# Opening of the trunk by pairs of channel tiles: one shift unit and one scale unit for each pair, and half weight blocks

## The chip, the cores and the metric

The kernel runs on one core of one Trainium2 chip. The metric is device microseconds of one execution, lower is better; the median of several runs is compared. Profiles come from one profiled execution. Engines: PE (TensorE, with PEld for its weight loads), DVE (VectorE), ACT (ScalarE), POOL (GpSimd) and SP (SyncE, which here only issues transfers).

## The reference

Two token groups (128 context tokens, 512 latent tokens) go through two layers. Only the opening of the first layer is touched:

```python
def layer(l, x, cvec, ctx_kv, ang):
    m = (jax.nn.silu(cvec) @ w_mod[l] + b_mod[l])[..., None, :]
    sh1, sc1, g1, sh2, sc2, g2 = jnp.split(m, N_MOD, axis=-1)
    h = _rmsnorm(x, norm1_g[l]) * (1 + sc1) + sh1
    q, k, v, bg, cg, xc = jnp.split(h @ w_in[l], SPLITS, axis=-1)
    q = _rmsnorm(q.reshape(bsz, n, N_HEADS, 2, HEAD_DIM), q_norm_g[l])
    ...
```

`D_MODEL` is 1024, that is, eight channel tiles of 128. `sh1` and `sc1` are the first two of six 1024-wide vectors that `w_mod` makes; `h` of a channel tile needs `sh1` and `sc1` of that tile.

## The kernel before

Each engine runs a program of its own, written out by hand in its final order, and they meet through counting semaphores (`wait_ge`, `then_inc`). Nothing is scheduled by a tool: what stands first on an engine runs first, and a wait holds all behind it.

All large products are made in float32 as three products of split numbers: a weight block is copied to `w_hi` by ACT (`split_hi_of`) and the rest, `raw - w_hi`, is written to `w_lo` by DVE (`split_lo_of`). A channel tile of `h` is split alike: DVE makes `hn` (x times gain times 1/rms, L1747), ACT adds the shift and makes `h_hi` (L1283), DVE makes `h_lo` (L1758). `norm_tiles(k0, k1)` does that for channel tiles k0 to k1-1 on DVE and `norm_hi(k)` on ACT. `h_ready` counts what is done, two steps to a tile.

`w_mod` comes in units of 256 columns (1 MB). Each unit covers two channel tiles. Units 0 to 3 make `sh1`, units 4 to 7 make `sc1`; they have their own buffers (`pre_w`, `mod_q`, by `PRE_SLOT`) and are loaded in the opening. A group of two units goes through these steps:

- PE: `mod_sum` for either unit, 8 matmuls each, into one PSUM bank (`mod_used` counts units);
- ACT: `rows`, the bank copied to `mod_row` (`row_read`);
- PE: `mod_turn`, four transposes back into the bank (`modT_full`);
- DVE: `mod_post`, a sum over four parts and the bias, into `modv` (`mod_ready`).

Before the change group 0 is units 0 and 1 (shift of channel tiles 0 to 3), group 2 is units 4 and 5 (scale of tiles 0 to 3), and groups 1 and 3 are the same for tiles 4 to 7. `PRE_ORDER` is 0, 2, 1, 3. Groups 0 and 2 are made before the first product; groups 1 and 3 between its steps.

The first product is the queries' part of `h @ w_in` (p = 0): 512 columns, five token tiles t, eight channel tiles k. `qkv_step` is three matmuls (L815 to L817) for one k and one t; five PSUM banks hold the sums of the five token tiles. Weight block 0 (slot 0) holds k = 0 to 3 and block 1 (slot 1) k = 4 to 7, 128x2048 each. For k = 0 to 3 the loop takes the five token tiles in turn. For k = 4 to 7 it takes t = 0 to 2, and then come whole `qkv_unit`s of four steps for t = 3 and t = 4. After k = 5 stands `first_pair_sum(0)`: the first two of the later `w_mod` units, from `mod_q`, with the row copy `rows(0, 0)` behind it on ACT and its turn (L729) between the units of t = 3 and t = 4. After t = 4 comes `first_pair_sum(1)`, whose first matmul waits until `mod_ready` is 5, that is, until DVE has made `mod_post(0, 0)`. On DVE that `mod_post` stands behind `split_lo(2)` (the keys' weight block 2) and behind the first item of the query norm (L1814 to L1845); on ACT the copy `split_hi(2)` stands behind `rows(0, 0)`. Then PE transposes `kc` (L883) and goes to the keys' part (p = 1).

Small rows (biases, gains, the convolution's weights, lambda and the rope tables) are issued by ACT's queue; PE transposes `vrow` and spreads `brow` (L795 to L798) before the first turn. POOL's queue loads the cached keys `kc` (L626), later the cached values, and in the MLP adds weight blocks (L636). SP's queue loads x, the `w_mod` units and the weight blocks in the order of its program.

## Time and profile before

| what | value |
|---|---|
| median of 3 runs | 1616.09 us (1615.43 to 1618.02) |
| profiled execution | 1615.98 us |
| its span, first to last instruction | 1614.2 us |
| PE busy | 1562.6 us, 97% |
| DVE busy | 1031.9 us, 64% |
| ACT busy | 727.3 us, 45% |
| mean granted TensorE clock | 0.99 |
| DMA in the first 40 us | 353 GB/s |

The profiled execution took 1.8 us more than its span. Times inside the trace are us from the span's start. The waits view says which engine stood idle and what ended it; the timeline gives, for merged rows, the start, the length, the engine and line, the tiles, the number of instructions, and in brackets the idle time before.

### The profile page before, as it was taken

How to read it: one execution, taken by the hardware profiler on the slowest of the kernel's cores; microseconds unless marked ns; L12 is line 12 of the kernel's file. 1: busy time of each engine (PE TensorE's matmuls, PEld its weight loads, DVE VectorE, ACT ScalarE, POOL GpSimd, SP SyncE). 2: the span in 40 equal slices, each digit the busy share in tenths (PEclk: the TensorE clock that was granted, in tenths of full speed). 3: DMA queues.
4: the chain of work that ended last, by engine and by line, in shares of the span. 5: the costliest groups of instructions: out<-in, count | busy, mean ns of one | idle time of the engine just before them, and what ended most of it. 6: DMA issues, size and time to landing. Idle time of an engine off the chain costs nothing. (4 is left out here: it accounts for less than half of the span.)

```text
span 1614.2 us, 26302 instructions
## 1 busy us (share of the span) xinstructions
PE 1562.6 (97%) x10543; PEld 1457.1 (90%) x10543; DVE 1031.9 (64%) x1654; ACT 727.3 (45%) x1216; POOL 142.6 (9%) x172
## 2 busy tenths in 40 slices
PE   5999999998999999999989999999899999999998
PEld 4777888987999999999977788889799999999998
DVE  5662666636775765757775537676587667476673
ACT  4543544325652643525443444533466355263451
POOL 0000000000211202112000000000022121120210
PEclk9999999999999999999989999999999999999999
DMA  9554011473866957759543531034088575694862
GB/s 353 183 189 164 27 53 35 149 253 87 190 150 151 216 136 167 180 150 219 156 147 111 170 105 53 28 104 131 3 196 186 146 184 147 160 211 135 193 152 82
DMA packets 284571, 236.13 MB, mean 146 GB/s; under 512 B 10464, under 2 KB 254752, under 8 KB 284448
## 3 DMA queue, kind: packets, MB, share of 16 engines
q1 hardware_dynamic: 259920, 189.82, 37.7%
q0 software_dynamic: 23680, 44.05, 15.9%
q8 instruction: 84, 1.38, 0.3%
q10 hardware_dynamic: 848, 0.56, 0.1%
q14 instruction: 39, 0.32, 0.1%
HBM read 188.78 MB, written 3.67 MB: 119 GB/s over the span
## 5 line engine op out<-in xcount | busy, mean ns | idle before, releaser
L636 POOL DMA_DIRECT2D raw_all<-raw_all x160 | 137.9, 877 | 1124.4 <-DMA raw_all<-in_w_up_dram 988.6
L1541 ACT ACTIVATE w_hi<-raw_all 128x1024 fp32r<-128x1024 f32 x120 | 126.1, 1056 | 234.9 <-DMA raw_all<-raw_all 116.1
L1154 PE MATMUL ps<-gg,w_hi 128*128 128x322 f32 x704 | 219.1, 311 | 0.0
L1156 PE MATMUL ps<-gg,w_lo 128*128 128x322 f32 x704 | 218.7, 311 | 0.0
L1155 PE MATMUL ps<-gg,w_hi 128*128 128x322 f32 x704 | 218.4, 310 | 0.0
L2077 DVE TENSOR_TENSOR w_lo<-raw_all,w_hi 128x1024 fp32r<-128x1024 f32 x120 | 146.5, 1221 | 109.8 <-ACT w_hi L1541 109.0
L1099 PE MATMUL ps<-hc_lo,w_hi 128*128 128x322 f32 x640 | 199.6, 312 | 0.0
L1101 PE MATMUL ps<-hc_hi,w_lo 128*128 128x322 f32 x640 | 198.9, 311 | 0.0
L1097 PE MATMUL ps<-hc_hi,w_hi 128*128 128x322 f32 x640 | 198.7, 310 | 0.0
L1097 PE MATMUL ps<-ht_hi,w_hi 128*128 128x322 f32 x480 | 150.7, 314 | 4.8 <-ACT s L1559 2.7
L1101 PE MATMUL ps<-ht_hi,w_lo 128*128 128x322 f32 x480 | 149.1, 311 | 0.0
L1099 PE MATMUL ps<-ht_lo,w_hi 128*128 128x322 f32 x480 | 149.0, 310 | 0.0
L1973 DVE SCALAR_TENSOR_TENSOR x<-ps,modv,x 128x128 f32<-128x128 f32 (+2 forms) x240 | 90.3, 433 | 91.5 <-PE ps L1156 54.1
L2038 DVE SCALAR_TENSOR_TENSOR tmp<-ub,vecs,tmp 128x642 f32<-128x642 f32 x168 | 139.3, 883 | 13.2 <-ACT tmp L1499 13.2
L1705 DVE TENSOR_TENSOR w_lo<-raw_all,w_hi 128x2048 fp32r<-128x2048 f32 x36 | 82.4, 2289 | 85.3 <-ACT w_hi L1267 85.3
L1156 PEld LDWEIGHTS ps<-gg,w_lo 128*128 128x128 f32 x704 | 132.9, 189 | 0.0
L1155 PEld LDWEIGHTS ps<-gg,w_hi 128*128 128x128 f32 x704 | 132.8, 189 | 0.0
L1154 PEld LDWEIGHTS ps<-gg,w_hi 128*128 128x128 f32 x704 | 132.5, 188 | 0.0
L686 PE MATMUL ps<-h_hi,w_hi 128*128 128x322 f32 x384 | 122.7, 320 | 0.0
L1097 PEld LDWEIGHTS ps<-hc_hi,w_hi 128*128 128x128 f32 x640 | 120.8, 189 | 0.0
L1101 PEld LDWEIGHTS ps<-hc_hi,w_lo 128*128 128x128 f32 x640 | 120.7, 189 | 0.0
L1099 PEld LDWEIGHTS ps<-hc_lo,w_hi 128*128 128x128 f32 x640 | 120.4, 188 | 0.0
(208 smaller groups left out, 3447.2 us busy)
## 6 DMA issues: line engine op xcount, KB each, us to landing
raw_all<-in_w_up_dram SPq DMA_DIRECT2D x280, 256.0 KB, 3.8
raw_all<-raw_all POOLq DMA_DIRECT2D x160, 256.0 KB, 4.0
raw_all<-in_w_in_dram SPq DMA_DIRECT2D x48, 512.0 KB, 4.8
raw_all<-in_w_mod_dram SPq DMA_DIRECT2D x48, 512.0 KB, 4.4
raw_all<-in_w_down_dram SPq DMA_DIRECT2D x16, 768.0 KB, 4.4
raw_all<-in_w_down_dram SPq DMA_DIRECT2D x16, 640.0 KB, 4.2
mod_q<-in_w_mod_dram SPq DMA_DIRECT2D x8, 1024.0 KB, 9.8
raw_all<-in_w_out_dram SPq DMA_DIRECT2D x16, 512.0 KB, 4.4
```

Source lines behind the costliest of these rows:

```text
L636: pool.dma_start(raw_f[:, BLK * dst:BLK * (dst + 1)], raw_f[:, BLK * src:BLK * (src + 1)], accum_op=ALU.add).then_inc(sum_full[which], 16)
L686: mm(out, wh[:, k, col:col + P], mov_hi(k), start=k == 0, stop=False)
L1097: mm(out, whi_f[:, c0:c0 + P], hh[:, k, slot, :], start=first and k == 0, stop=False, skip_group_check=not first)
L1099: mm(out, whi_f[:, c0:c0 + P], hl[:, k, slot, :], start=False, stop=False, skip_group_check=not first)
L1101: ins = mm(out, wlo_f[:, c0:c0 + P], hh[:, k, slot, :], start=False, stop=k == KH - 1, skip_group_check=not first)
L1154: mm(out, wh[:, k, :], gh, start=k == 0, stop=False)
L1155: mm(out, wh[:, k, :], gl, start=False, stop=False)
L1156: ins = mm(out, wl[:, k, :], gh, start=False, stop=k == kf - 1)
L1541: A(whi_b[:, 2 * i:2 * (i + 1), :], src, ACT.Copy).then_inc(up_hi[i], 1)
L1973: ins = V.scalar_tensor_tensor(out=xs, in0=ps[:, banks[h], p0:p0 + n], scalar=gate, in1=xs, op0=ALU.mult, op1=ALU.add)
L2038: return V.scalar_tensor_tensor(out=cen[:, s, 1:T - 1], in0=u[:, s, j:j + T - 2], scalar=vecs[:, l, w:w + 1], in1=cen[:, s, 1:T - 1], op0= ...
L2077: V.tensor_tensor(wlo_b[:, pair, :], raw_b[:, pair, :] if i else first_pair(g), whi_b[:, pair, :].bitcast(F32), ALU.subtract).then_inc(up_ ...
```

## The change

- The four opening groups are now by pairs of channel tiles: group h is unit h (shift) and unit 4 + h (scale) of tiles 2h and 2h + 1, all in one bank. `first_post(h)` on DVE takes the place of `mod_post` for them: two sums, one bias add.
- Only group 0 is made before the first product. Groups 1 to 3 have their sums after t = 2 of k = 0, 2, 4, and their turns after t = 1 of k = 1, 3, 5. Gains and `norm_tiles` go by two tiles.
- Weight block 0 comes as two halves (`first_part`), each split on its own (`part_split_hi`, `part_split_lo`, 128x1024); the first step needs only the first half.
- k = 0 to 5 take all five token tiles. For k = 6 and 7 the token tiles 0 to 2 come first, then `first_pair_sum(0)`, then tiles 3 and 4, the turn, and `first_pair_sum(1)`.
- Eight small rows stay on ACT's queue. Ten (convolution of the MLP, lambda, query and key gains) and the rope tables go to POOL's queue, ahead of `kc`; rope there waits for `hh_ready` 4.
- ACT loads the Sqrt table early, squares the context tokens before the latent ones have come, and makes the lambda exponential after all eight tiles.

```diff
-PRE_ORDER = [0, 2, 1, 3]
-PRE_BANKS = {0: 7, 2: 1, 1: 7, 3: 7}
-PRE_SLOT = {0: 0, 1: 2, 4: 1, 5: 3, 2: 4, 3: 5, 6: 6, 7: 7}
+PRE_SLOT = {0: 0, 4: 2, 1: 1, 5: 3, 2: 4, 6: 5, 3: 6, 7: 7}
...
             pre_load(0)
+            pre_load(4)
+            first_part(0)
             pre_load(1)
-            for u in (4, 5):
-                pre_load(u)
-            load(0, w_in_v, 0, KH, 0, QC)
-            for u in (2, 3, 6, 7):
-                pre_load(u)
+            pre_load(5)
+            first_part(1)
+            pre_load(2)
+            pre_load(6)
             load(1, w_in_v, KH, KH, 0, QC)
+            pre_load(3)
+            pre_load(7)
...
+            pool.wait_ge(const_ready, 2)
+            for l in range(DEPTH):
+                fr = ffn_conv_w[l].rearrange("w (t n) -> (w t) n", n=P)
+                pool.dma_start(vrow[:, l, 1, :], fr[0:P, :]).then_inc(rows_in, 16)
+                pool.dma_start(vrow[0:3 * V_FT - P, l, 2, :], fr[P:3 * V_FT, :]).then_inc(rows_in, 16)
+            for i, src in enumerate((lambda_q1, lambda_k1, lambda_q2, lambda_k2, q_norm_g, k_norm_g)):
+                pool.dma_start(brow[0:1, i * P:(i + 1) * P], src.rearrange("(a l) n -> a (l n)", a=1)
+                               ).then_inc(rows_in, 16)
+            pool.wait_ge(hh_ready, 4)
+            pool.dma_start(rope[:, :, :, :], rope_in).then_inc(rope_full, 16)
...
-            pre_sum(0)
+            mod_sum(None, 0, 0, None, None)
...
+            mod_sum(None, 0, 1, None, None)
+            spread(0, 0)
             mod_turn(None, 0)
-            pre_sum(2)
-            spread(0, 0)
-            mod_turn(None, 2)
...
+                    for k in range(KT - 2):
...
+                        for t in range(NT):
+                            normed(k, t)
+                            ins = qkv_step(k // KH, t, k % KH)
+                            if k % 2 == 0 and t == 2:
+                                pre_sum(k // 2 + 1)
+                            elif k % 2 and t == 1:
+                                mod_turn(None, k // 2 + 1)
...
+                    for t0, t1 in ((0, 3), (3, NT)):
+                        for k in range(KT - 2, KT):
+                            for t in range(t0, t1):
...
+                        if t0 == 0:
+                            first_pair_sum(0)
                     mod_turn(l, 0)
-                qkv_unit(1, 4)
-                first_pair_sum(1)
+                    first_pair_sum(1)
...
+            A(junk[:, 1:2], eps[:, :], ACT.Sqrt)
...
+            def first_post(h):
+                dve.wait_ge(modT_full, h + 1)
+                turned = ps[:, MOD_BANK, :].rearrange("p (v t q m) -> p v t m q", v=2, q=4, m=QUAD)
+                for vec in range(2):
+                    V.tensor_reduce(modv[:, vec, 2 * h:2 * h + 2, :], turned[:, vec, :, 0:2, :], axis=AX.X, op=ALU.add)
+                dve.drain()
...
-                    norm_tiles(4, KT)
+                    for k in range(0, KT, 2):
+                        if k:
+                            first_post(k // 2)
+                            dve.drain()
+                        gains(0, V_N1, k, k + 2)
+                        dve.drain()
+                        norm_tiles(k, k + 2)
+                        if k == 0:
+                            part_split_lo(1)
+                        elif k == 2:
+                            split_lo(1)
```

On PE, at the start of the first product, the rows before are these (the sums of groups 0 and 2 with the setup between them; L718 is a sum, L729 a turn, L750 the spread of 1/rms, L815 the first step):

```order
L718 MATMUL ps<-pre_w,cT 32x256 [waits pre_full0,cT_ready]
...
L718 MATMUL ps<-pre_w,cT 32x256 [waits pre_full1]
...
L795 MATMUL ps<-ident,vrow 128x128 [waits xT_read,ffn_in,small_in]
...
L729 MATMUL ps<-ident,mod_row 128x128 [waits row_read]
...
L718 MATMUL ps<-pre_w,cT 32x256 [waits pre_full4]
...
L718 MATMUL ps<-pre_w,cT 32x256 [waits pre_full5]
...
L815 MATMUL ps<-w_hi,h_hi 128x512 [waits h_ready,split_full0]
```

and with the change these (L733 is a sum, L744 a turn, L829 the first step):

```order
L733 MATMUL ps<-pre_w,cT 32x256 [waits pre_full0,cT_ready]
...
L810 MATMUL ps<-ident,vrow 128x128 [waits xT_read,rows_in,small_in]
...
L733 MATMUL ps<-pre_w,cT 32x256 [waits pre_full4]
...
L744 MATMUL ps<-ident,mod_row 128x128 [waits row_read]
...
L829 MATMUL ps<-w_hi,h_hi 128x512 [waits h_ready,part_lo]
...
L733 MATMUL ps<-pre_w,cT 32x256 [waits pre_full1,mod_ready]
```

One group of sums and one turn have gone behind the first step, and the setup's transposes wait for POOL's rows.

On PE, at the end of the queries' part, the rows before run from `first_pair_sum(0)` over 30 matmuls (k = 6 and 7 of t = 0 to 2, and the unit of t = 3), the turn and 12 matmuls (the unit of t = 4) to `first_pair_sum(1)` and the transposes of `kc` (L883):

```order
L718 MATMUL ps<-mod_q,cT 32x256 [waits mod_ready,modq_full0]
...
L729 MATMUL ps<-ident,mod_row 128x128 [waits row_read]
...
L815 MATMUL ps<-w_hi,h_hi 128x512
...
L718 MATMUL ps<-mod_q,cT 32x256 [waits mod_ready,modq_full2]
...
L883 MATMUL ps<-ident,kc 128x128 [waits kv_in]
```

and with the change only the steps of t = 3 and 4 (12 matmuls) and the turn stand between the two sums:

```order
L733 MATMUL ps<-mod_q,cT 32x256 [waits mod_ready,modq_full0]
...
L829 MATMUL ps<-w_hi,h_hi 128x512 [waits h_ready]
...
L744 MATMUL ps<-ident,mod_row 128x128 [waits row_read]
L744 MATMUL ps<-ident,mod_row 128x128 x3
L733 MATMUL ps<-mod_q,cT 32x256 [waits mod_ready,modq_full2]
...
L913 MATMUL ps<-ident,kc 128x128 [waits kv_in]
```

42 matmuls of the product stood between the two sums, 12 do now; the other 30 are ahead of the first sum.

On ACT the rows around `rows(0, 0)` before are

```order
L1217 ACTIVATE mod_row<-ps 128x512 [waits mod_used]
L1267 ACTIVATE w_hi<-raw_all 128x2048 [waits unit_done0,raw_full0]
L1326 ACTIVATE sq<-ps 128x512 [waits qkv_full]
L1329 ACTIVATE qraw<-ps 128x512
L1331 ACTIVATE st<-st,eps 128x8 [waits qsum_ready]
```

and with the change

```order
L1332 ACT_TABLE_LOAD
L1332 ACTIVATE lam_s<-lam_s 128x4 [waits lam_ready]
L1333 ACT_TABLE_LOAD
L1333 ACTIVATE junk<-eps 128x1
L1246 ACTIVATE mod_row<-ps 128x512 [waits mod_used]
L1290 ACTIVATE w_hi<-raw_all 128x2048 [waits unit_done0,raw_full0]
L1358 ACTIVATE sq<-ps 128x512 [waits qkv_full]
```

The copy of weight block 2 still stands behind the row copy; the lambda exponential and its two table loads have come in front of both.

## Rows read from the trace of the kernel before

**Rows 1.** Page, part 1: busy time, share and count of instructions.

```profile
PE 1562.6 (97%) x10543; PEld 1457.1 (90%) x10543; DVE 1031.9 (64%) x1654; ACT 727.3 (45%) x1216; POOL 142.6 (9%) x172
```

**Rows 2.** Waits of PE, 100 to 1614 us: total, times, longest.

```profile
PE ps L937 <- ACT probs L1386: 4.7, 4, 1.4
```

**Rows 3.** Timeline of PE before the first product: start, length, instruction, count.

```profile
18.66 0.88 PE L795 MATMUL ps<-ident,vrow 128*128 128x128 f32 x6
...
20.95 0.66 PE L729 MATMUL ps<-ident,mod_row 128*128 128x128 f32 x4
...
24.07 1.60 PE L750 MATMUL ps<-sq,ones 128*128 128x128 f32 x12
25.52 0.60 PE L729 MATMUL ps<-ident,mod_row 128*128 128x128 f32 x4
32.65 0.77 PE L815 MATMUL ps<-w_hi,h_hi 128*128 128x512 f32 x1 [6.53 <-DVE h_lo L1758]
```

**Rows 4.** Timeline of DVE: last opening memset, copies of x, first tiles.

```profile
2.37 0.06 DVE L1663 MEMSET eps<- 128x1 f32 x1
...
13.50 3.08 DVE L1678 COPY x<-ps 128x512 f32<-128x512 f32 x5
...
26.15 0.19 DVE L1650 TENSOR_REDUCE modv<-ps 128x8 f32<-128x32 f32 x1 [2.59 <-PE ps L729]
...
27.04 1.13 DVE L1747 SCALAR_TENSOR_TENSOR hn<-x,gain,ps 128x128 f32<-128x128 f32 x3
...
31.11 1.12 DVE L1747 SCALAR_TENSOR_TENSOR hn<-x,gain,ps 128x128 f32<-128x128 f32 x3
```

**Rows 5.** Page, part 5: a half block's low part, and a transfer issued by POOL.

```profile
L636 POOL DMA_DIRECT2D raw_all<-raw_all x160 | 137.9, 877 | 1124.4 <-DMA raw_all<-in_w_up_dram 988.6
...
L2077 DVE TENSOR_TENSOR w_lo<-raw_all,w_hi 128x1024 fp32r<-128x1024 f32 x120 | 146.5, 1221 | 109.8 <-ACT w_hi L1541 109.0
```

**Rows 6.** Line L626 (POOL's load of kc), last line of the answer.

```profile
DMA to landing us min/median/max: 6.6/6.6/6.6
```

**Rows 7.** Windows: length, busy time of PE, PEld, DVE, ACT, POOL, clock, DMA share, GB/s.

```profile
26.20:32.60 6.40, 0.00 (x0) 0.00 (x0) 5.43 (x18) 3.55 (x5) 0.00 (x0) 0.70 1.09 353
32.60:35.60 3.00, 2.95 (x7) 2.41 (x8) 3.00 (x8) 1.70 (x4) 0.00 (x0) 0.50 1.09 348
```

**Rows 8.** Timeline of PE in the first product.

```profile
50.06 0.60 PE L729 MATMUL ps<-ident,mod_row 128*128 128x128 f32 x4
...
54.13 0.47 PE L815 MATMUL ps<-w_hi,h_hi 128*128 128x512 f32 x1 [0.69 <-DVE h_lo L1758]
...
58.49 1.93 PE L718 MATMUL ps<-mod_q,cT 128*32 128x256 f32 x32
...
67.41 0.60 PE L729 MATMUL ps<-ident,mod_row 128*128 128x128 f32 x4
...
70.74 1.93 PE L718 MATMUL ps<-mod_q,cT 128*32 128x256 f32 x32
```

**Rows 9.** Timeline of ACT: the row copy of the first pair sum, and weight block 2.

```profile
60.49 0.60 ACT L1217 ACTIVATE mod_row<-ps 128x512 f32<-128x512 f32 x1 [2.08 <-PE ps L718]
60.99 1.91 ACT L1267 ACTIVATE w_hi<-raw_all 128x2048 fp32r<-128x2048 f32 x1
```

**Rows 10.** Timeline of DVE: weight block 2, mod_post(0, 0) and mod_post(0, 1).

```profile
62.93 2.29 DVE L1705 TENSOR_TENSOR w_lo<-raw_all,w_hi 128x2048 fp32r<-128x2048 f32 x1 [2.88 <-ACT w_hi L1267]
...
68.69 0.17 DVE L1653 TENSOR_TENSOR modv<-modv,vecs 128x8 f32<-128x8 f32 x1
...
77.86 0.17 DVE L1653 TENSOR_TENSOR modv<-modv,vecs 128x8 f32<-128x8 f32 x1
```

**Rows 11.** Timeline of PE, 366 to 378 us: two units' sums at half clock, then at full.

```profile
369.93 3.49 PE L718 MATMUL ps<-mod_t,cT 128*32 128x256 f32 x32
...
374.97 1.93 PE L718 MATMUL ps<-mod_x,cT 128*32 128x256 f32 x32
```

**Rows 12.** Timeline of PE: the keys' part, its first sum.

```profile
79.62 1.07 PE L718 MATMUL ps<-raw_all,cT 128*32 128x256 f32 x16
```

More of the change, by code:

```diff
@@ L183 @@
 HALVES = 24
-N_SMALL = 15
+N_SMALL = 8
+N_ROWS = 10
 YT_BANKS = [6, 7, 0, 1, 3, 4, 2, 5, 6, 7]
@@ L189 @@
 MOD_BANK = 7
-PRE_ORDER = [0, 2, 1, 3]
-PRE_BANKS = {0: 7, 2: 1, 1: 7, 3: 7}
-PRE_SLOT = {0: 0, 1: 2, 4: 1, 5: 3, 2: 4, 3: 5, 6: 6, 7: 7}
+PRE_SLOT = {0: 0, 4: 2, 1: 1, 5: 3, 2: 4, 6: 5, 3: 6, 7: 7}
 def mod_bank(l, h):
-    if l is None:
-        return PRE_BANKS[h]
-    return 2 if h == GAP_A[l] + 1 else MOD_BANK
+    return 2 if l is not None and h == GAP_A[l] + 1 else MOD_BANK
 LAM_INIT = [0.8 - 0.6 * math.exp(-0.3 * i) for i in range(DEPTH)]
@@ L867, in _ @@
-                pe.wait_ge(split_full[1], usable(l, 1))
-                for k in range(KH, KT):
-                    for t in range(3):
-                        normed(k, t)
-                        ins = qkv_step(1, t, k - KH)
-                        if k == KT - 1:
-                            ins.then_inc(qkv_full, 1)
-                    if l == 0 and k == 5:
-                        first_pair_sum(0)
-                qkv_unit(1, 3)
-                if l == 0:
-                    mod_turn(l, 0)
@@ L1224, in _ @@
             act.wait_ge(const_ready, 2)
-            small = [(rope[:, :, :, :], rope_in)]
+            small = []
             for src, r0, n in ((b_mod, V_BMOD, 48), (norm1_g, V_N1, KT), (norm2_g, V_N2, KT),
@@ L1231, in _ @@
                               conv_w[:, j, :].rearrange("l (t n) -> t l n", n=P)))
-            for i, src in enumerate((lambda_q1, lambda_k1, lambda_q2, lambda_k2, q_norm_g, k_norm_g)):
-                small.append((brow[0:1, i * P:(i + 1) * P], src.rearrange("(a l) n -> a (l n)", a=1)))
             assert len(small) == N_SMALL
             A(junk[:, 0:1], eps[:, :], ACT.Silu)
-            for dst, src in small[:8]:
+            for dst, src in small:
                 act.dma_start(dst, src).then_inc(small_in, 16)
@@ L1267, in split_hi_of, with part_split_hi @@
                 A(w_hi[:, b, 0:size], raw[:, b, 0:size], ACT.Copy).then_inc(hi_done[b], 1)
+            def part_split_hi(s):
+                act.wait_ge(part_in[s], 16)
+                A(w_hi[:, 0, s * 2 * QC:(s + 1) * 2 * QC], raw[:, 0, s * 2 * QC:(s + 1) * 2 * QC], ACT.Copy
+                  ).then_inc(hi_done[0] if s else part_hi, 1)
             rows(None, 0)
-            rows(None, 2)
-            split_hi_of(0, 0)
+            part_split_hi(0)
             for l in range(DEPTH):
@@ L1289, in _ @@
                     norm_hi(k)
-                    if k == 3:
-                        if l == 0:
-                            rows(None, 1)
+                    if l == 0 and k == 1:
+                        part_split_hi(1)
+                        rows(None, 1)
+                    elif l == 0 and k == 3:
                         split_hi(1)
-                        if l == 0:
-                            act.wait_ge(lam_ready, 1)
-                            A(lam_s[:, :], lam_s[:, :], ACT.Exp).then_inc(lam_exp, 1)
-                            A(junk[:, 0:1], eps[:, :], ACT.Sqrt)
-                            rows(None, 3)
+                        rows(None, 2)
+                    elif l == 0 and k == 5:
+                        rows(None, 3)
+                    elif l and k == 3:
+                        split_hi(1)
                     elif l and k == 5:
@@ L1301, in _ @@
                 if l == 0:
+                    act.wait_ge(lam_ready, 1)
+                    A(lam_s[:, :], lam_s[:, :], ACT.Exp).then_inc(lam_exp, 1)
+                    A(junk[:, 0:1], eps[:, :], ACT.Sqrt)
                     rows(l, 0)
@@ L1715, in _ @@
             dve.drain()
-            mod_post(None, 0)
             for l in range(DEPTH):
@@ L1725, in _ @@
                             ).then_inc(lam_ready, 1)
-            mod_post(None, 2)
+            first_post(0)
             for l in range(DEPTH):
@@ L1737, in reciprocals, with part_split_lo @@
                     reciprocals_of(l, which)
+                def part_split_lo(s):
+                    dve.wait_ge(hi_done[0] if s else part_hi, 1)
+                    part = slice(s * 2 * QC, (s + 1) * 2 * QC)
+                    V.tensor_tensor(w_lo[:, 0, part], raw[:, 0, part], w_hi[:, 0, part].bitcast(F32), ALU.subtract
+                                    ).then_inc(split_full[0] if s else part_lo, 1)
                 def norm_tiles(k0, k1):
```

119 lines of the change are left out of this document (62 added, 57 removed).

## Prediction

> **What bounds the kernel now.** The page first: PE is busy 97% of the span, no other engine over 64% [rows 1]. So the time is PE's work plus PE's idle time, and each idle stretch has to be read for what ended it. In the waits of PE after 100 us all ten kinds are ended by ACT or DVE, none by a DMA; the kind that comes back below is one of the attention, 4.7 us in four waits [rows 2]. A delay put in early is therefore carried to the end, unless such a wait takes it up. The opening is where PE idles most: after its last turn at 25.52 it has nothing until the first step at 32.65, 6.53 us [rows 3]. The windows show what this does to the clock: the granted share falls to 0.70 within the idle 6.4 us, and the next 3.0 us run at 0.50 (1.2 GHz), 7 matmuls in 2.95 us, 0.42 each, where the pace at full clock is 0.233 [rows 7].
>
> That pace I take from the timeline of the product: the sum of `first_pair_sum(0)` starts at 58.49, lasts 1.93 (to 60.42), 30 matmuls fill the time to the turn at 67.41, so 6.99 / 30 = 0.233; and turn plus 12 matmuls take 70.74 - 67.41 = 3.33 us [rows 8].
>
> **The change, part by part.**
>
> *An earlier first step.* PE can begin the setup (transposes of small rows) when DVE has copied x, at 13.50 + 3.08 = 16.58, say 16.7 [rows 4]; before it began at 18.66, behind the second unit's sum. Setup to turn is 20.95 - 18.66 = 2.29 [rows 3], which gives 19.0. The scale unit's sum (half of 1.93, 0.97) ends at 20.0; the spread takes 25.52 - 24.07 = 1.45, ACT's row copy of 0.60 lies beside it; the turn (0.60) ends at 22.0 [rows 3, 8]. From DVE's first sum at 26.15 to the first step at 32.65 were 6.50 us. In them, between `hn` of tile 0 (27.04 + 1.13 = 28.17) and of tile 1 (31.11), lay 2.94 us for the low part of a whole weight block [rows 3, 4]. Half a block costs 1.22 [rows 5], 1.72 less; the extra short sum adds about 0.19 [rows 4]. 6.50 - 1.72 + 0.19 = 4.97, so the first step comes at 27.0: **-5.65 us**. PE idles 5.0 us before it, little less than 6.53, so I let the half clock behind it cost what it cost before.
>
> *The small rows.* PE asks for them at 16.7. POOL may start after DVE's memsets, at 2.5 [rows 4], and issues ten; at 0.877 us an issue, as in its other transfers [rows 5], the last is issued at 10.4, and at the 6.6 us that `kc` took to land in this same busy stretch [rows 6] it is there at 17.0: 0.3 us late, not added above. The bounds: nothing if they land faster; if the issues cost 1.3 us instead, the last lands at 2.5 + 9 x 1.3 + 6.6 = 20.8, 4.1 us late, and all behind it with it. I stay at nothing, since `kc` (128x512) is four times as large as the largest of them (128x128). What is queued behind on POOL (rope, `kc`) is wanted only at DVE's rope tables and at PE's transposes after 72 us.
> The Trainium skill (DMA: Bandwidth & Descriptors, Anatomy of one DMA) gives a GpSimd transfer 2.0 us plus its bytes at 436 GB/s; an estimate from that page puts the last row at 12.6 and this term at zero. It would give `kc` 2.6 us; the trace has 6.6, so here the rule is not what bounds it.
>
> *One more group inside the product.* Three groups' sums and turns now lie behind the first step, two before: 1.93 for the sums, 3.33 - 12 x 0.233 = 0.53 for the turn, **+2.5 us** [rows 8].
>
> *Waits at the borders of the pairs.* A turn started at 50.06 and the first step that needed it at 54.13: 4.07 us of bias add, gains, two `hn`, `h_hi` and the first `h_lo`, covered by 12 matmuls, with 0.69 idle left [rows 8]. The change has this path three times (before k = 2, 4, 6), 0.1 longer for the second short sum, and covers each with the turn (0.53) and 9 matmuls (2.10) only: 4.17 - 2.63 = 1.5 idle, three times 4.6. Before were 0.69 and 0.20 (the latter is a bank's wait that goes too): **+3.7 us**.
>
> So PE would ask for `first_pair_sum(1)` at 70.74 - 5.65 + 2.5 + 3.7 = **71.3**: the gain at the front is already given back, with 0.6 on top.
>
> *The new wait.* `first_pair_sum(1)` waits for `mod_post(0, 0)`. Its chain is: sum (0, 0) ends at 60.42; ACT copies the row at 60.49 and weight block 2 at 60.99 for 1.91 [rows 9]; DVE takes the low part at 62.93 for 2.29, the first query item, and the bias add at 68.69 + 0.17 = 68.86 [rows 10]. That is 8.44 us. Before, 42 matmuls and a turn covered it (60.42 to 70.74, 10.3 us) and 1.9 us were left over. Now 12 matmuls and the turn stand there, 3.33 us [rows 8]. Queued behind the waiting matmul is the whole keys' part. The lambda exponential moved ahead on ACT is free: ACT has nothing else until the row. So PE waits 8.44 + 0.1 - 3.33 = **5.2 us** and starts the sum at 76.5, 5.8 later than 70.74.
>
> *Half clock behind it.* PE idled 6.53 us before and came back at 0.50; 5.2 us is near that, so I expect the same. Two units' sums took 3.49 at half clock and 1.93 at full, with the clock the only difference in the rows [rows 11]: **+1.5 us**. Whether some matmuls behind it are slow too is left to the range (7 were before, 0.2 each, 1.4). If the clock stays, the next check is `mod_post(0, 1)`: it ended at 78.03, 9.17 behind `mod_post(0, 0)` [rows 10], so now at 85.6, and PE asks for it at 79.62 + 5.8 = 85.4 [rows 12]: the delay is then 6.0, not less.
>
> **Sum:** -5.65 + 2.5 + 3.7 + 5.2 + 1.5 = +7.3 us. Against the profiled execution (1615.98, its span 1614.2 and 1.8 around it) that is 1623.3; the median of the runs is 0.1 higher, and on it I forecast **1623.4 us**.
>
> **The rivals.**
>
> 1. *The clock stays full after the new wait.* For it: 5.2 us is shorter than the idle time that lowered it. Against: the clock fell inside the 6.4 us window and not at its end [rows 7]. +6.0, 1622.1 us.
> 2. *The small rows come late* and the new bound of the opening is POOL's queue. For it: no row of before shows ten issues of POOL in a row. Against: the sizes. At 1.3 us an issue +7.3 + 4.1 = +11.4, 1627.5 us. The Trainium skill (SBUF — State Buffer, SBUF: two separate sides) says that DVE in a two-port mode keeps GpSimd from writing descriptors; no row here shows it, and it would be this rival's cause.
> 3. *Not slower: the attention takes the delay up.* PE waits there for ACT's exponentials, 4.7 us over both layers [rows 2]. If ACT's work in those places were late from its own backlog and not released by PE, a delay of PE would shrink these waits, at most by 4.7: +2.6, 1618.7 us. It decides only if nearly all of it is taken up, 4.1 of 4.7. Against: half of it lies in the second layer, and those exponentials follow PE's own scores.
> 4. *The change doesn't do what it says*, and the pairs' waits don't appear, because DVE gets through the path in less than 2.6 us: -4.6 in the forecast. The new wait stays, since its chain starts at the first sums: it moves with PE, so +2.7, 1618.8 us. Against: 4.07 us is measured. With no half clock too it would be faster than that by 1.5, and with some of rival 3 faster than before.
>
> **How the numbers follow.** Forecast 0.62, rival 1 0.14, rival 2 0.10, rival 3 0.06, rival 4 0.05, faster than before by any sum of these 0.03. Measurement tells 0.2%, 3.2 us, from no change. Slower: 0.62 + 0.14 + 0.10 = 0.86; same 0.11; faster 0.03. The range takes rival 1 and leaves room below it for a first step 1 to 2.5 us earlier than my 27.0, down to 1619.8, and takes rival 2 above: to 1627.8.
>
> **What would show it.** In the trace after: PE's first step near 27 (26 to 28), idle before it about 5; waits of about 1.5 before k = 2, 4 and 6, ended by DVE `h_lo`; one wait of about 5.2 on `modv` at about 71, with the bias add 8.4 behind the first sums; half clock behind it; `kc`'s transposes at about 80 in place of 72.6. Wrong at the front if PE waits for a DMA of `vrow` or `brow`; wrong at the end if PE passes `first_pair_sum(1)` with no wait, in which case I would find 1618 or less.

## The result, and the profile after

The changed kernel takes 1622.47 us (median of 7 executions, 1619.54 to 1626.92), the kernel before 1615.43 (7 executions): ratio 1.0046, 95% interval 1.0034 to 1.0058. The change costs 7.0 us. The forecast was 1623.4, slower by 7.3 than the median of 1616.1 known then.

The page of the changed kernel, its span and part 1 (compare [rows 1]):

```profile
span 1620.3 us, 26321 instructions
...
PE 1563.8 (97%) x10543; PEld 1457.4 (90%) x10543; DVE 1033.2 (64%) x1661; ACT 726.9 (45%) x1218; POOL 148.5 (9%) x183
```

Span less PE's busy time is 56.5 us; before it was 1614.2 - 1562.6 = 51.6. PE does the same 10543 matmuls, and 4.9 of the 6.1 us in the span are idle time. The waits of PE, 0 to 110 us (total, times, longest), say where:

```profile
PE ps L829 <- DVE h_lo L1806: 8.8, 4, 4.7
PE ps L793 <- DMA ident<-in_ident_dram: 8.8, 1, 8.8
PE ps L733 <- DVE modv L1695: 5.2, 1, 5.2
PE ps L810 <- DVE x L1720: 0.9, 1, 0.9
```

Behind 100 us nothing new waits; the attention's line of [rows 2] reads

```profile
PE ps L967 <- ACT probs L1418: 4.7, 4, 1.4
```

as before, so it took nothing up. The timeline of PE (start, length, instruction, count, idle before), for [rows 3], [rows 8] and [rows 12]:

```profile
17.49 0.84 PE L810 MATMUL ps<-ident,vrow 128*128 128x128 f32 x6 [0.89 <-DVE x L1720]
...
19.75 1.76 PE L733 MATMUL ps<-pre_w,cT 128*32 128x256 f32 x16
21.43 2.53 PE L765 MATMUL ps<-sq,ones 128*128 128x128 f32 x12
23.80 0.60 PE L744 MATMUL ps<-ident,mod_row 128*128 128x128 f32 x4
29.10 0.77 PE L829 MATMUL ps<-w_hi,h_hi 128*128 128x512 f32 x1 [4.71 <-DVE h_lo L1806]
...
42.21 0.47 PE L829 MATMUL ps<-w_hi,h_hi 128*128 128x512 f32 x1 [1.34 <-DVE h_lo L1806]
...
53.34 0.47 PE L829 MATMUL ps<-w_hi,h_hi 128*128 128x512 f32 x1 [1.44 <-DVE h_lo L1806]
...
64.41 0.51 PE L829 MATMUL ps<-w_hi,h_hi 128*128 128x512 f32 x1 [1.31 <-DVE h_lo L1806]
...
68.79 1.93 PE L733 MATMUL ps<-mod_q,cT 128*32 128x256 f32 x32
...
73.54 0.60 PE L744 MATMUL ps<-ident,mod_row 128*128 128x128 f32 x4
79.30 3.64 PE L733 MATMUL ps<-mod_q,cT 128*32 128x256 f32 x32 [5.16 <-DVE modv L1695]
82.87 1.12 PE L913 MATMUL ps<-ident,kc 128*128 128x128 f32 x4
```

The new wait stands at 74.14, 5.16 us long. DVE's side of it, for [rows 10], with the end of the setup for [rows 4]:

```profile
24.43 0.25 DVE L1675 TENSOR_REDUCE modv<-ps 128x4 f32<-128x16 f32 x2 [2.42 <-PE ps L744]
...
26.43 1.22 DVE L1784 TENSOR_TENSOR w_lo<-raw_all,w_hi 128x1024 fp32r<-128x1024 f32 x1
...
73.22 2.29 DVE L1747 TENSOR_TENSOR w_lo<-raw_all,w_hi 128x2048 fp32r<-128x2048 f32 x1 [6.36 <-ACT w_hi L1290]
...
78.98 0.17 DVE L1695 TENSOR_TENSOR modv<-modv,vecs 128x8 f32<-128x8 f32 x1
```

From the end of the first pair's sum (68.79 + 1.93 = 70.72) to 79.15 are 8.43 us. The windows (length, busy times, clock, DMA share, GB/s), for [rows 7], show the clock in the setup, in the first idle time and behind either wait:

```profile
17.40:20.00 2.60, 2.51 (x16) 1.47 (x20) 1.92 (x9) 0.00 (x0) 0.00 (x0) 1.00 1.09 385
20.00:23.40 3.40, 3.40 (x25) 2.38 (x18) 1.84 (x6) 1.54 (x2) 0.00 (x0) 0.50 1.09 393
```

```profile
24.40:29.10 4.70, 0.00 (x0) 0.03 (x1) 4.42 (x19) 1.90 (x4) 0.00 (x0) 0.76 1.09 360
29.10:33.30 4.20, 4.20 (x13) 2.88 (x17) 2.67 (x4) 1.29 (x2) 1.12 (x2) 0.50 1.07 386
...
79.30:84.80 5.50, 5.50 (x39) 3.28 (x40) 5.21 (x15) 2.04 (x5) 0.54 (x1) 0.50 0.16 56
```

**More is lost early than at the end.** The same instruction of both traces, three times: at the attention's first wait, in the output product of the first layer, and of the second. Before:

```profile
196.59 1.35 PE L937 MATMUL ps<-kT,qT 64*128 64x128 f32 x7 [0.98 <-ACT probs L1386]
```

```profile
389.24 0.42 PE L1073 MATMUL ps<-hc_hi,w_hi 128*128 128x322 f32 x1 [1.64 <-DVE hc_lo L2019]
```

```profile
1170.14 0.41 PE L1073 MATMUL ps<-hc_hi,w_hi 128*128 128x322 f32 x1 [1.63 <-DVE hc_lo L2019]
```

After:

```profile
207.75 1.34 PE L967 MATMUL ps<-kT,qT 64*128 64x128 f32 x7 [0.99 <-ACT probs L1418]
```

```profile
396.95 0.41 PE L1103 MATMUL ps<-hc_hi,w_hi 128*128 128x322 f32 x1 [1.62 <-DVE hc_lo L2069]
```

```profile
1175.62 0.41 PE L1103 MATMUL ps<-hc_hi,w_hi 128*128 128x322 f32 x1 [1.63 <-DVE hc_lo L2069]
```

The delay is 11.2 us, then 7.7, then 5.5. It began as two nearly equal parts: up to the point where the keys' part is under way (85 us before, 96.2 after, 470 matmuls in either) PE is busy for 66.85 and 72.56 us, so 5.7 us of the delay are slower matmuls and 5.5 us are idle time. Behind that point PE is idle for 33.4 us before and 32.9 after, so waits took up at most 0.5 us of it. The rest came back by the clock: the kernel before runs two stretches of PE at half clock, here in its windows,

```profile
295.10:298.40 3.30, 3.30 (x15) 3.30 (x14) 2.90 (x8) 2.50 (x3) 0.00 (x0) 0.50 0.02 5
370.20:373.50 3.30, 3.30 (x33) 1.45 (x25) 1.26 (x7) 0.34 (x2) 0.00 (x0) 0.50 0.00 0
```

and the changed kernel has the full clock from 290 to 400 us:

```profile
290.00:400.00 110.00, 104.42 (x826) 94.85 (x825) 61.42 (x117) 42.39 (x70) 0.35 (x1) 1.00 0.50 161
```

Half clock costs half of the 3.3 us of each window, so the two are 3.3 of the 3.5 us between the first and the second pair of rows. Of the next 2.2, 1.75 lie in the windows from 815 to 850 us, 0.80 against 0.85 of the full clock over 35 us:

```profile
815.00:850.00 35.00, 30.36 (x166) 25.50 (x165) 25.96 (x64) 14.19 (x23) 0.57 (x1) 0.80 0.28 90
```

```profile
815.00:850.00 35.00, 30.36 (x189) 26.68 (x188) 25.59 (x63) 15.70 (x23) 0.57 (x1) 0.85 0.44 142
```

(before, then after). By the end of the trace the difference is 6.1 us, the two spans' difference.

### The profile page after: what moved, and what is told of

The parts are those of the page before. It is cut to its first block and busy times, and to the rows that moved or that the text cites. A ratio compares the mean times of both kernels' runs of the same rounds, so it can differ in the third digit from the quotient of the medians.

```text
span 1620.3 us, 26321 instructions
## 1 busy us (share of the span) xinstructions
PE 1563.8 (97%) x10543; PEld 1457.4 (90%) x10543; DVE 1033.2 (64%) x1661; ACT 726.9 (45%) x1218; POOL 148.5 (9%) x183
```

## The experiments

Each is compared with executions of the kernel before on the same chip and in the same batch. The batches differ (the median of the kernel before is 1614.9 to 1617.2 in them), so kernels of different batches are compared by their ratios, not by their medians. PE's idle time is the span less its busy time in each trace; the clock is the mean of the granted share over all timed executions. The two rows that start with "and" add to "chain and turns early", the second of them to the first.

| kernel | ratio, 95% interval | median, us | PE idle, us | PE busy, us | clock |
|---|---|---|---|---|---|
| before | 1 | 1614.9 to 1617.2 | 51.6 | 1562.6 | 0.9907 (0.9904 to 0.9914 by batch) |
| changed | 1.0046 (1.0034 to 1.0058) | 1622.5 | 56.5 | 1563.8 | 0.9894 |
| changed, again | 1.0050 (1.0031 to 1.0068) | 1622.2 | 55.3 | 1564.8 | 0.9895 |
| before, end changed | 1.0042 (1.0030 to 1.0054) | 1622.5 | 56.4 | 1563.3 | 0.9892 |
| bias add first | 1.0049 (1.0035 to 1.0064) | 1624.2 | 54.7 | 1560.7 | 0.9903 |
| turns early | 1.0041 (1.0029 to 1.0053) | 1621.1 | 52.2 | 1569.7 | 0.9876 |
| both | 1.0038 (1.0025 to 1.0051) | 1622.0 | 52.4 | 1570.1 | 0.9884 |
| chain early | 1.0024 (1.0004 to 1.0043) | 1620.2 | 52.8 | 1562.8 | 0.9895 |
| chain and turns early | 1.0005 (0.9991 to 1.0019) | 1616.2 | 49.2 | 1564.3 | 0.9895 |
| and low part early | 0.9995 (0.9982 to 1.0009) | 1614.8 | 49.1 | 1563.6 | 0.9902 |
| and three moves more | 0.9982 (0.9971 to 0.9992) | 1614.3 | 50.3 | 1563.8 | 0.9910 |
| rows on ACT | 1.0053 (1.0037 to 1.0070) | 1624.3 | 56.4 | 1564.0 | 0.9892 |
| idle time filled | 1.0048 (1.0029 to 1.0067) | 1623.3 | 51.5 | 1565.2 | 0.9917 |
| filled, again | 1.0044 (1.0027 to 1.0061) | 1622.3 | 50.7 | 1569.4 | 0.9917 |

### One part alone: the new end in the kernel before

```diff
-                for k in range(KH, KT):
-                    for t in range(3):
...
-                    if l == 0 and k == 5:
-                        first_pair_sum(0)
-                qkv_unit(1, 3)
...
+                    for k in range(KH, KT - 2):
+                        for t in range(NT):
...
+                    for t0, t1 in ((0, 3), (3, NT)):
...
+                        if t0 == 0:
+                            first_pair_sum(0)
+                    mod_turn(l, 0)
```

> The kernel before, with only the end of the queries' part taken from the change: k = 4 and 5 with all five token tiles, k = 6 and 7 with t = 0 to 2, then first_pair_sum(0), t = 3 and 4, the turn and first_pair_sum(1). Theory (the new wait comes from that order alone): 12 matmuls and a turn, 3.3 us, stand against a chain of 8.4, so PE waits about 5.1 us for mod_post(0, 0), the sums behind it run at half clock (3.5 instead of 1.93), and the median rises by 5 to 7 us over the kernel before. Rival (the wait needs the opening by pairs, or a delay here is taken up later): PE waits under 2 us, or the median rises by under 3 us.

Ratio 1.0042, 6.8 us. Its timeline of PE has the wait and the half clock behind it to the hundredth of those in the changed kernel:

```profile
76.89 3.64 PE L718 MATMUL ps<-mod_q,cT 128*32 128x256 f32 x32 [5.16 <-DVE modv L1665]
```

The theory holds. This order alone costs as much as the whole change; the opening by pairs, with its first step 3.6 us earlier and its extra group and border waits, gains nothing in sum.

### The bias add first, the turns early, and both

The first kernel moves one call on DVE:

```diff
+                    mod_post(l, 0)
                 split_lo(2)
...
                         if t == 1 and p == 0:
-                            if l == 0:
-                                mod_post(l, 0)
                             rope_tables()
```

> The changed kernel, with DVE's mod_post(0, 0) ahead of split_lo(2) and of the first query item instead of behind them; all else as changed. Theory (the new wait is DVE's order, and it and the half clock behind it go through to the end): the bias add comes about 0.6 us behind the turn (which ends at 74.14), so the wait of 5.16 us falls to about 0.6, the sums of first_pair_sum(1) take 1.93 instead of 3.64, the transposes of kc come about 6.5 earlier (76.3 instead of 82.87), and the median falls by 6 to 7 us, to about 1616. Rival A (a delay at 75 us is taken up later, as the smaller shift of later stages in the trace suggests): the wait goes, but the median falls by under 3 us, to 1620 or more. Rival B (the wait only moves): a wait of 2 us or more appears on the keys' part, because split_lo(2) now comes 2 us later, and the median stays above 1618.

The second moves the three turns:

```diff
-                            elif k % 2 and t == 1:
+                            elif k % 2 == 0 and t == 4:
                                 mod_turn(None, k // 2 + 1)
```

> The changed kernel, with the turns of groups 1 to 3 behind t = 4 of k = 0, 2, 4 instead of behind t = 1 of k = 1, 3, 5, two steps earlier (ACT has copied the row 2.1 us before the turn starts in each of the three cases). Theory (the waits at the pairs' borders are the path of about 4.1 us less its cover of 2.6): the cover becomes 2 steps, 1.4 us, longer; the waits of 1.34, 1.44 and 1.31 us before k = 2, 4, 6 fall to 0.1 or less each, the new wait of 5.16 stays since its chain moves with PE, and the median falls by about 4 us, to 1618.5. Rival (these short waits cost nothing in the end, or the row copy becomes the next late thing): PE waits at the turn for ACT's mod_row, or the median falls by under 2 us.

The third has both.

> Both edits: mod_post(0, 0) ahead of split_lo(2), and the three turns two steps earlier. Theory (the two losses are independent and go through to the end): the gains add up, 6.7 + 4.1 = 10.8 us, to about 1611.7, which is 4 us faster than the kernel before. Rival A (later stages take up what is delayed at 80 us): the sum is much less than the parts, and the median stays at 1615 or above, no faster than before.

All three stay between 1.0038 and 1.0049. With the bias add first PE's timeline reads

```profile
72.72 1.93 PE L733 MATMUL ps<-mod_q,cT 128*32 128x256 f32 x32 [0.62 <-DVE modv L1695]
```

```profile
82.05 0.86 PE L744 MATMUL ps<-ident,mod_row 128*128 128x128 f32 x4 [4.01 <-ACT mod_row L1246]
```

The wait fell to 0.62 as expected, and 4.01 us came at the next turn: rival B, at another place than I named. ACT makes that row behind query items 0 to 2, and DVE's work on items 0 and 1 stands before it. (The trace is of the shortest execution, 1617.2 us; the other five lie from 1623.0 to 1625.3.) The expected 6 to 7 us were not gained: the ratio is 1.0049. So `mod_post(0, 0)` was not the only thing late but the first in one chain: weight block 2, query items, row (0, 1), `mod_post(0, 1)`.

With the turns early the borders' waits went (PE has one wait of 4.7 for `h_lo` left in place of four of 8.8 in sum), and idle time fell by 4.3 us, as the theory said. The median is lower by 1.2 only, which is also what the rival named (under 2 us). The page of the kernel with both shows the rest:

```profile
span 1622.5 us, 26321 instructions
...
PE 1570.1 (97%) x10543; PEld 1462.7 (90%) x10543; DVE 1033.4 (64%) x1661; ACT 726.2 (45%) x1218; POOL 148.3 (9%) x183
```

Its idle time is 52.4 us, nearly that of before, but the same matmuls take 7.5 us longer: they run at half clock for longer. A window holds one such stretch, which begins inside the wait for ACT's row (75.98 to 80.00) and goes on behind it:

```profile
78.40:85.10 6.70, 5.10 (x16) 4.42 (x17) 6.29 (x14) 4.13 (x7) 0.00 (x0) 0.50 0.00 0
```

### The chain early, with and without the turns

```diff
-                    rows(l, 0)
-                split_hi(2)
+                    split_hi(2)
+                    rows(l, 0)
...
                         if t == 0:
+                            if l == 0 and p == 0:
+                                rope_tables()
                             group_sums(n)
+                            if l == 0 and p == 0:
+                                mod_post(l, 0)
```

With the turns early as well:

> The changed kernel with the turns two steps earlier, and with the query norm's chain on ACT and DVE started earlier: ACT copies weight block 2 ahead of the row (0, 0), DVE makes the rope tables ahead of the first query item, and mod_post(0, 0) behind that item's first sum. In the run with both edits PE lost the 5.2 us at first_pair_sum(1) but then waited 4.02 us for ACT's row copy of pair (0, 1), which stands behind two query items that DVE makes. Theory (one chain, DVE's query items from split_lo(2) on, stands behind both waits): with the chain 4 to 5 us earlier both go, at most 1 us of idle is left between 65 and 90 us, no half clock lies there, and the median falls from 1622.0 by 4.0 for the wait and 2 for the clock, to 1616, level with the kernel before. Rival (the chain meets yet another thing, or the clock costs elsewhere what it gives back here): a wait over 1.5 us appears at another place before 95 us, or the median stays at 1619 or above.

Ratio 1.0005, 1616.2 us; 1616 was expected. PE's waits in the first 110 us:

```profile
PE ps L793 <- DMA ident<-in_ident_dram: 8.9, 1, 8.9
PE ps L829 <- DVE h_lo L1808: 4.7, 1, 4.7
PE ps L733 <- DVE modv L1697: 1.6, 2, 1.0
```

The waits of 5.2 and 4.0 us are gone, no wait over 1.5 us has come up elsewhere, and the clock is full from 60 to 95 us. Of the chain 1.6 us in two waits are left, and 0.57 us for ACT's `qT`, where at most 1 us was expected. By the ratios (1.0041 with the turns alone) three moved calls gain 5.8 us, with some 3 us of uncertainty. With the turns and the bias add alone the ratio is 1.0038, so the gain comes from the rest of the chain, block 2 and the rope tables; these two were not moved one at a time. The same without the early turns:

> The changed kernel with the earlier query chain alone (block 2 ahead of the row copy on ACT, rope tables and mod_post(0, 0) earlier on DVE); the turns stay where the change has them, behind t = 1 of k = 1, 3, 5. Against the kernel with chain and early turns (1.0005 of the kernel before) it prices the three waits at the pairs' borders by themselves. Theory (each of the three waits goes through to the end, since all that follows, DVE's chain too, starts from PE's steps): waits of 1.3 to 1.4 us before k = 2, 4 and 6 are back, no wait above 1 us between 65 and 80 us, and the ratio to the kernel before is higher by 4.1 us, 1.0030. Rival (with the turns early alone the median fell by 1 to 2 us only, not 4, so the early turns are worth little on their own and most of the gain is the chain's): the ratio is 1.0015 or less.

Ratio 1.0024, against 1.0030 for the theory and at most 1.0015 for the rival. The waits came out as expected (1.31 us before k = 6, none above 0.62 between 65 and 80 us), but the interval holds both ratios, so this run does not decide what the waits at the borders are worth. The difference to 1.0005 is 3.1 us for 4.1 us of waits, and the two intervals overlap. That the turns alone gave only 1.2 us fits their clock: 0.9876, the lowest of all, is 2.9 us worse than 0.9894, and 4.3 less 2.9 is 1.4. This is an account, not a test: why the clock was lower there is not shown.

### The low part early, and three moves more

```diff
+            dve.wait_ge(part_hi, 1)
+            V.tensor_tensor(w_lo[:, 0, 0:2 * QC], raw[:, 0, 0:2 * QC], w_hi[:, 0, 0:2 * QC].bitcast(F32), ALU.subtract
+                            ).then_inc(part_lo, 1)
             first_post(0)
...
-                        if i == 0 and l == 0:
-                            part_split_lo(0)
```

> As the kernel with the earlier chain, and in the opening DVE makes the low part of the first half block ahead of first_post(0), in the idle time of 2.42 us that it has there, instead of between the first two hn. Theory (DVE's path from the first turn to the first step sets the first step): the first step comes 1.1 to 1.2 us earlier (29.1 to 27.9), the idle time before it is 3.5 us, and the median is 1 to 2 us under that of the kernel with the chain alone, about 1614.5. Rival (the first step then waits for something else, or the time is lost again at the next pair's border): the first step moves by under 0.6 us, or the wait before k = 2 grows by as much.

Ratio 0.9995; the median is 1.4 us under that of the kernel with the chain and the turns, inside the expected 1 to 2, with overlapping intervals. But the first step moved by 0.42 us only (27.78 to 27.36, both with full clock in the setup), which is what the rival named (under 0.6), and the idle time before it is 4.34 us and not 3.5, since DVE began the low part too late:

```profile
22.69 1.23 DVE L1770 TENSOR_TENSOR w_lo<-raw_all,w_hi 128x1024 fp32r<-128x1024 f32 x1 [0.45 <-ACT w_hi L1295]
```

It ended at 23.9, and the turn at 23.0. The last kernel mends that and two more places:

```diff
+            act.wait_ge(mod_used, 1)
+            part_split_hi(0)
             rows(None, 0)
-            part_split_hi(0)
...
                 if l == 0:
+                    split_hi(2)
                     act.wait_ge(lam_ready, 1)
...
-                    split_hi(2)
                     rows(l, 0)
```

> As the kernel with the earlier chain and the early low part, with three more moves: ACT copies the first half block ahead of the row of group 0 (it stands idle for 4.5 us there), so DVE makes its low part before the lambda sums and not 0.8 us into the time that the turn has already ended; ACT copies weight block 2 ahead of the lambda exponential and its two table loads (3.0 us), with DVE's neglam behind split_lo(2); and mod_post(0, 0) stands behind the scaling of query item 0. Theory (two chains on DVE set the time: turn to first step, and split_lo(2) with the query items up to mod_post(0, 1)): the idle time before the first step falls from 4.34 to 3.6 us, split_lo(2) starts at about 60.5 in place of 63.35, the waits of 0.96 and 0.58 us behind 76 us go, and the median falls by 1.5 to 2.5 us under the kernel with the early low part, to 1612.5 to 1613.5, below the kernel before by 0.1%. Rival (the query items are no longer what is late and half clock decides the rest): the median stays within 0.7 us of 1614.8.

Ratio 0.9982 (0.9971 to 0.9992), faster than both kernels: 0.18%, 2.9 us, against the kernel before. Its first step and block 2 on DVE:

```profile
27.97 0.77 PE L829 MATMUL ps<-w_hi,h_hi 128*128 128x512 f32 x1 [3.57 <-DVE h_lo L1811]
```

```profile
62.04 2.29 DVE L1750 TENSOR_TENSOR w_lo<-raw_all,w_hi 128x2048 fp32r<-128x2048 f32 x1 [0.74 <-ACT w_hi L1290]
```

The idle time before the first step is the 3.6 us expected, and the wait of 0.96 us on `modv` in the keys' part is gone; the one of 0.58 on ACT's `qT` is not, against the theory. Block 2 came 1.5 us later than expected in a trace that has half clock in its setup. PE's idle time in the whole trace did not fall against the kernel with the low part alone: it is 50.3 and not 49.1 us, since 1.7 us less of waits up to 110 us stand against more behind (ACT's `s` in the MLP 3.4 in place of 2.3 us, weights 1.0 in place of 0.2). The median is 1614.3 against 1614.8, within the 0.7 us that the rival named; by the ratios it is 2.1 us lower, but the intervals overlap. So a gain over that kernel is not shown; a gain over the kernel before is.

### The small rows back on ACT's queue

```diff
-                pool.dma_start(vrow[:, l, 1, :], fr[0:P, :]).then_inc(rows_in, 16)
...
+                act.dma_start(vrow[:, l, 1, :], fr[0:P, :]).then_inc(rows_in, 16)
```

> The changed kernel with the ten small rows back on ACT's queue, behind the Silu, as before; the rope tables stay on POOL's queue. Theory (the small rows are on nobody's path, on either queue): the ten issues take ACT about 3 us (0.3 each, as before), the squares and the square root end at about 19 in place of 16.6, still before the spread that needs them at 21.4; the first step stays within 0.4 us of 29.1 and the median within 1 us of 1622.3. Rival (POOL's queue delays the opening's other transfers, of which the identity landed 0.44 us later than before): the first step comes 0.4 us or more earlier and the median falls by as much. Rival 2 (the rows on POOL's queue are what made an earlier setup possible): the setup's transposes start 1 us or more later than 17.5 and the median rises by that.

The setup's transposes start at 17.60 in place of 17.49, the first step at 27.64 in place of 29.10. So the step moved by more than the 0.4 us of the theory. The queue does not explain it: this trace has full clock in the setup, as four traces with the rows on POOL's queue have too (first step at 27.5 to 27.8 in the three whose path is the same), and the idle time before the step is 4.73 us, as in the changed kernel. The identity landed 0.2 us earlier. The median did not fall, as the rival had it: it is 1624.3, and the ratio 1.0053, whose interval holds 1.0046. No cost or gain of the queue shows in these runs.

### The changed kernel again, and with its idle time filled

> The changed kernel once more, unchanged, for a second trace of it. In the first trace PE's shift against the kernel before is 11.2 us from 85 to 290 us and 6.2 us at the end, and the stretches at half clock behind 290 us lie in other places than in the trace before. Theory A (the early loss is fixed; what is given back behind 290 us is only where the half clock happens to fall in one execution): the waits before 80 us have the same lengths within 0.1 us (4.7, 1.3, 1.4, 1.3, 5.2), and the stretches at half clock behind 290 us lie elsewhere again. Theory B (later waits take up some of the delay for good): the half clock lies where it lay, and the shift at the end is 6 us again. Median 1622.5 on either.

The ratio is 1.0050. The median is 1622.2. Theory A is right on the waits (8.9 us for `h_lo` and 5.2 for `modv`, as in the first trace) and wrong on the clock: from 290 to 400 us the second trace has the full clock too,

```profile
290.00:400.00 110.00, 104.18 (x825) 94.61 (x825) 61.22 (x117) 42.11 (x69) 0.31 (x1) 1.00 0.51 162
```

and its row of the output product starts at 396.92, within 0.03 us of the first. Theory B named the outcome (6 us at the end), and in part its reason too. Up to 397 us what came back is clock, in both traces. Behind that they differ: the second trace has a further stretch at half clock at 1160 us, so its row of the second layer starts at 1177.78, 7.6 us behind the kernel before and not 5.5, and the last 1.7 us came back behind that row. Behind it PE is idle for 7.9 us, against 9.7 in the first trace and 9.0 in the kernel before; its waits for ACT's `s` in the MLP are 0.7 us in sum, against 2.0 and 1.3. So later waits can be shorter in one execution than in the next, by 1 to 2 us here.

Nor does the delay alone decide where the half clock falls. The kernel with the chain and the turns early and the last kernel reach the attention's first wait at 196.76 and 196.71, and the kernel before at 196.59. The first has both stretches of the kernel before, the second has neither:

```profile
290.00:400.00 110.00, 104.58 (x803) 93.75 (x802) 62.40 (x118) 43.62 (x67) 2.65 (x3) 0.97 0.54 169
```

```profile
290.00:400.00 110.00, 103.84 (x820) 94.21 (x819) 64.53 (x120) 44.92 (x67) 2.64 (x3) 1.00 0.57 173
```

So the 3.3 us that came back by 397 us are a fact of these traces, not something that follows from the delay.

```diff
+                    for _ in range(10):
+                        mm(ps[:, 0, :], w_hi[:, 0, 0:P], w_hi[:, 0, 0:QC], start=True, stop=True)
...
                     mod_turn(l, 0)
+                    for _ in range(18):
+                        mm(ps[:, 5, :], h_hi[:, 7, C_PROMPT:C_PROMPT + P], w_hi[:, 1, 0:QC], start=True, stop=True)
                     first_pair_sum(1)
```

> The changed kernel with matmuls of no use (128x512 of the product's kind, results overwritten or never read) in two of PE's idle stretches: 10 before the first step and 18 before first_pair_sum(1). The idle time there was 4.71 and 5.16 us, and they take 2.3 and 4.2 us at full clock, so nothing is put off. Theory (the idle time lowers the clock behind it): the first nine matmuls of the product take 0.23 each and not 0.43, the sums behind the wait 1.93 and not 3.64, kc's transposes 0.66 and not 1.12, so about 2.0 + 2.2 = 4 us come back, and the median is about 1618.5. Rival (the clock falls there by something else than the idle time): half clock remains behind at least one of the two, and the median stays above 1621.

> The kernel with the filling matmuls once more, unchanged, since its trace and its median disagree: in the trace PE runs at full clock up to 373 us and the profiled execution took 1618.5 us, as expected, but the median of the timed executions was 1623.3. Theory A (the idle time sets the clock, and the first median was scatter; single executions lay between 1618.5 and 1628.0): the second median is below 1621, and the trace shows again full clock up to 90 us. Theory B (with the idle time filled the clock still falls in most executions, somewhere else): the second median is 1622 or above again, and the trace shows stretches at half clock behind 90 us that make up for those that went, 13 us or more in sum over the two traces' mean.

In the first of the two traces the clock did what the theory says:

```profile
26.99 0.47 PE L829 MATMUL ps<-w_hi,h_hi 128*128 128x512 f32 x1 [2.38 <-DVE h_lo L1812]
```

```profile
75.18 1.93 PE L733 MATMUL ps<-mod_q,cT 128*32 128x256 f32 x32 [0.94 <-DVE modv L1701]
```

The sums take 1.93 us, not 3.64, and the profiled execution took 1618.5 us. But the medians are 1623.3 and 1622.3, on the changed kernel's own. The mean clock of the timed executions did rise, from 0.9894 to 0.9917, or 3.7 us over 1620; about half of that lies in the filled idle time itself (1.75 us in the changed kernel's first trace), where a low clock had cost nothing. So neither theory is whole: filling raised the clock, and no time came back that these runs can tell. Next to the changed kernel's 1.0046 and 1.0050, their intervals leave hardly room for a gain of 4 us, but do for one of 2. A part of the loss can be seen. PE now meets waits in the keys' part that the changed kernel has not:

```profile
84.38 1.07 PE L733 MATMUL ps<-raw_all,cT 128*32 128x256 f32 x16 [0.25 <-DVE modv L1701]
...
89.41 0.63 PE L933 MATMUL ps<-ident,qn 128*128 128x128 f32 x4 [0.58 <-ACT qT L1355]
```

From the end of the wait on `modv` to the second sum of the keys' part PE takes 17.57 us filled (75.18 to 92.75) and 19.10 in the changed kernel (79.30 to 98.40), 1.5 us less and not the 2.6 of the clock. PE's idle time is 51.5 and 50.7 us, where 28 matmuls of 0.233, 6.5 us, in the changed kernel's 56.5 or 55.3 would leave 50.0 or 48.8. The second trace has half clock in the setup and at 302 us and again at 834 (page: PE busy 1569.4), the first at 373 and 834. But the kernel without filling has such stretches behind 90 us too, at 832 and later ones, so that what went in front came up again behind, as theory B has it, is not shown. Where the rest goes stays open.

## Why the prediction was right, and where only by a balance

*First step: 29.10, not 27.0.* The front gained 3.55 us, not 5.65, and this step failed. The path from the turn was right: idle 4.71 us where I said 5.0, and the turn to first step took 29.10 - 24.40 = 4.7. The setup before it was late by 2.4 us. I took each of its pieces at the pace of before; here the second unit's sum took 1.76 us and the spread 2.53, where 0.97 and 1.45 were in my sum, since PE ran at half clock from 20.0 to 23.4 while it was busy all the time. That is 1.9 us; the copies of x ended 0.8 later than I had taken them. In the four traces with full clock there and the same path from the turn, the first step comes at 27.5 to 27.8, still 0.5 to 0.8 us behind 27.0 and inside the 26 to 28 that the prediction named as its sign.

*The small rows: nothing.* POOL's issues took 0.48 to 0.70 us, not 0.88, and the last landed within 5.7 us of an issue at 7.48, so at 13.2, 4 us before the transposes asked for them at 17.4. Rival 2 is out, and the kernel with the rows on ACT's queue agrees. The Trainium skill (DMA: Bandwidth & Descriptors, Anatomy of one DMA) gives 2.0 us and the bytes' time; the rows' 5.3 to 5.9 us from issue to landing are above that, as [rows 6] had said.

*Groups and borders.* Three waits of 1.34, 1.44 and 1.31 against three of 1.5; the net was 3.2, not 3.7. Rival 4 is out.

*The new wait: 5.16 against 5.2*, with a chain of 8.43 against 8.44. PE asked at 74.14, not at 71.3: 2.1 from the front, 0.8 since nine matmuls and part of a sum were slow behind the first step and not seven matmuls, 0.5 back at the borders, and 0.4 in small pieces.

*Half clock behind it: 1.71 against 1.5* for the sums. The range's term came too: `kc`'s transposes and three matmuls ran slow, 0.9 us more. Rival 1 is out, at least for the two traces of this kernel and the one of before with the new end. The Trainium skill (TensorE: Matmul & The Clock Gate, HAM oscillation — how this bites in real kernels) prices a stretch at the lower rate at half its length; 3.64 less 1.93 is 47% of 3.64, so the trace agrees.

*The sum.* At 85 us the delay was 11.2 us, not 7.3: those 2.8 us and 0.2 and 0.9 from the clock behind the wait. Then 3.5 us came back by 390 us and 2.2 more by 1170, nearly all by half clock that the trace of before has and this one has not. I had said that a delay is carried to the end unless a wait takes it up, and had left the clock out of that. So the forecast of +7.3 met +7.0, but two errors of 4 and 5 us stand against each other in it, and that they balance is luck. Over the timed executions the account is 4.9 us more idle time, from one trace of each, and (0.9907 - 0.9894) x 1620 = 2.1 us of clock; as the clock of the kernel before is 0.9904 to 0.9914 by batch, the second term is known to about 1 us only, and the exact sum of 7.0 is chance.

*Rival 3* (the attention takes it up): 4.7 us in four waits, as before. Out.

*Not seen.* I took the bias add for the end of the chain. I checked the next wait, `mod_post(0, 1)`, for the delayed kernel only, not for one without the delay. With the bias add first, PE waited 4 us for the row of pair (0, 1) as soon as it no longer waited before it.

## What to carry to other kernels

When a wait ends on an engine that works through a chain (here weight block, norm items, bias add), moving one late item to the front can just move the wait to the next item. Find the first instruction of the chain and what holds it (here a copy on ACT that stood behind a row that PE made late), and move that. And read a small change against idle time and mean clock apart: of 7 us here 5 were idle time; in the kernel with both early edits nearly none were, and it was as slow.

## What was not expected of the hardware

The clock stands at 0.50 while PE is busy all the time: 3.40 of 3.40 us from 20.0 to 23.4, on short sums and 128x128 matmuls, behind 2.6 us at full clock with 2.51 busy and one wait of 0.89 just ahead of those. Five of the ten traces with the opening by pairs and no filling show this, and the other five run the same work at full clock. In the kernel before PE ran at 0.50 for 3.3 us at 295 and at 370 with no idle time in it, behind waits of 0.20 us (at 291.6) and 0.55 us (at 368.7) only. Neither trace of the changed kernel has these two stretches, but the last kernel, with no delay against the kernel before, has not got them either, and the kernel with both early edits, 6.6 us behind at 197 us, has them. What decides where such stretches fall is not settled by these runs. For the same 10543 matmuls PE's busy time lies between 1560.7 and 1570.1 us in the table, a spread of 9.4 us and more than most edits of an opening are worth.
